# One-hots of the gate matrix in a PEER routing stage: from two engines with 8 tokens a batch to one engine with 16

## The reference, cut to what matters

```
q = (xb @ wq).reshape(PEER_BLOCK, PEER_HEADS, 2, PEER_DHALF)
s = jnp.einsum('thcd,hcnd->thcn', q, subkeys)            # 2 x 128 scores
sv, si = lax.top_k(s, PEER_TOPK)                         # 16 best of each half
cand = sv[:, :, 0, :, None] + sv[:, :, 1, None, :]
fv, fi = lax.top_k(cand, PEER_TOPK)                      # 16 best pairs
i1 = take_along_axis(si[:, :, 0], fi // PEER_TOPK)
i2 = take_along_axis(si[:, :, 1], fi % PEER_TOPK)
e = i1 * N_KEYS + i2                                     # expert number
g = jax.nn.softmax(fv, axis=-1)
a = jax.nn.gelu(jnp.einsum('thkd,td->thk', u_tab[e], xb))
y = jnp.einsum("thk,thkd->td", g * a, v_tab[e])
```

## Time and profile before

| what | value |
|---|---|
| median of 3 runs | 4247.77 us (4244.9 to 4252.57) |
| the profiled execution | 4249.34 us |
| its span | 4247.5 us |
| routing stage in the span | about 1096 to 1959 us |
| experts stage in the span | from 1959 us to the end |

### The profile page before, as it was taken

The page is one execution under the profiler, slowest core; times in us unless marked ns, Lnnn a source line. Parts: engine busy times, 40 slices in busy tenths (PEclk is TensorE's granted clock), DMA queues, the critical chain, the costliest instruction groups (busy, mean ns, idle before and its releaser), DMA issues.

```text
span 4247.5 us, 54962 instructions
## 1 busy us (share of the span) xinstructions
PE 3343.3 (79%) x20744; PEld 1998.0 (47%) x20744; DVE 2474.5 (58%) x4984; ACT 730.5 (17%) x1124; POOL 1327.8 (31%) x1103
## 2 busy tenths in 40 slices
PE   5899665888766566552778888889997899998998
PEld 2555552444665555541444344445453544444454
DVE  3110454443278888885877666666665666664445
ACT  2111232111001122221111121112121212111111
POOL 0000000000000333331554545554545465543442
PEclk8899776999877666666999999999999999999999
DMA  6211334322300222117888888898887898887882
GB/s 182 82 54 68 107 110 170 102 102 101 121 11 11 84 85 65 51 49 246 294 289 283 287 278 280 304 314 299 316 299 277 310 326 319 315 306 250 314 312 101
DMA packets 335811, 836.25 MB, mean 197 GB/s; under 512 B 43513, under 2 KB 148897, under 8 KB 331361
## 3 DMA queue, kind: packets, MB, share of 16 engines
q0 software_dynamic: 129024, 469.82, 31.8%
q1 hardware_dynamic: 206576, 363.62, 24.8%
HBM read 741.40 MB, written 93.19 MB: 196 GB/s over the span
## 4 chain that ended last, share of the span: by engine, by line
PE 23%; DMA 11%; DVE 6%; POOL 4%; DVEq 4%; issue 3%; SPq 1%; ACT 1%; POOLq 0%; ACTq 0%
PE experts_ps L1508 11%; PE experts_ps L1494 8%; DMA experts_ut<-in_uT 6%; DMA experts_v_rows<-in_v,picks_by_choice 5%; PE experts_ps L1525 4%; POOL experts_u_rows L1600 2%; DVEq L1712 2%; POOL experts_v_rows L1613 2%; DVE experts_ul L1646 2%; DVEq L1682 1%; DVE experts_hl L1685 1%; DVE experts_prod L1711 1%; ACT experts_uh L1552 1%; DVE experts_hf L1681 1%; DVE experts_hh L1683 1%
## 5 line engine op out<-in xcount | busy, mean ns | idle before, releaser
L1600 POOL DMA_INDIRECT experts_u_rows<-in_u_rows,picks_by_token x448 | 576.1, 1286 | 776.1 <-DVEq L1712 684.9
L1494 PE MATMUL experts_ps<-experts_xh,experts_uh 128*128 128x320 f16 x2048 | 614.5, 300 | 56.5 <-DMA experts_xl<-scratch_xl 27.2
L1494 PE MATMUL experts_ps<-experts_xh,experts_ul 128*128 128x320 f16 x2048 | 614.0, 300 | 0.0
L1494 PE MATMUL experts_ps<-experts_xl,experts_uh 128*128 128x320 f16 x2048 | 614.0, 300 | 0.0
L1508 PE MATMUL experts_ps<-experts_vh,experts_hh 128*128 128x512 f16 x1280 | 500.5, 391 | 99.9 <-issue 87.7
L1613 POOL DMA_INDIRECT experts_v_rows<-in_v,picks_by_choice x448 | 498.4, 1113 | 248.7 <-issue 125.9
L1711 DVE CUSTOM_DVE_ANT_0 experts_prod<-experts_u_rows,experts_x 128x1024 f16<-128x1024 f32 x448 | 545.8, 1218 | 24.8 <-issue 12.4
L1508 PE MATMUL experts_ps<-experts_vl,experts_hh 128*128 128x512 f16 x1280 | 498.6, 390 | 0.0
L1508 PE MATMUL experts_ps<-experts_vh,experts_hl 128*128 128x512 f16 x1280 | 496.8, 388 | 0.0
L1696 DVE SCALAR_TENSOR_TENSOR experts_y<-experts_ps,experts_y 128x512 f32<-128x512 f32 x320 | 221.0, 691 | 471.0 <-PE experts_ps L1508 458.3
L1525 PE MATMUL experts_ps<-experts_v_rows,experts_sel 128*32 128x512 f32 x1792 | 269.8, 648 | 131.7 <-DMA experts_v_rows<-in_v,picks_by_choice 129.3
(11 more groups left out here) (257 smaller groups left out, 5050.4 us busy)
## 6 DMA issues: line engine op xcount, KB each, us to landing
experts_ut<-in_uT SPq DMA_DIRECT2D x128, 512.0 KB
experts_vt<-in_v SPq DMA_DIRECT2D x128, 512.0 KB, 6.2
scratch_g<-route_gbuf SPq DMA_DIRECT2D x5, 8192.0 KB, 30.6
experts_g<-scratch_g SPq DMA_DIRECT2D x128, 320.0 KB, 4.8
scratch_z<-project_z SPq DMA_DIRECT2D x10, 1984.0 KB, 7.1
project_piece<-in_w_in SPq DMA_DIRECT2D x15, 1024.0 KB, 5.8
merge_w_piece<-in_w_merge SPq DMA_DIRECT2D x13, 1024.0 KB, 7.8
mix_za<-scratch_z SPq DMA_DIRECT2D x10, 960.0 KB, 5.6
```

What stands on the lines that cost most here:

```text
L1494: mm = pe.matmul(ps[:, A0 + k2 % 2, 0:W], w[:, e % 2, k, :], x[:, k, c * W:(c + 1) * W], start=k == 0 and j == 0, stop=k == KT - 1 and j == 2)
L1600: pool.indirect_dma_start(u_rows[:, k % RU], None, u_table, bass.IndirectOffsetOnAxis(ap=picks.by_token[:, b, j:j + 1], axis=0)).then_inc( ...
```

## The change

VectorE makes all four one-hot matrices of a batch. A batch has 16 tokens in four groups, so every operation has 2048 elements in each partition instead of 1024, a block has 8 batches instead of 16, and the loop goes round twice instead of four times. `hot_h` is gone: after `hot_l` is made from `hot_r`, `hot_r` is multiplied by `gh` in place. GpSimd has nothing left to do in this stage. A batch now fills all four PSUM banks (4 to 7), and the order in which banks are reused is the old one. In `top16` match-and-replace writes over the scores instead of into `rest`, which is gone. Semaphore counts follow the new sizes.

```diff
-BT, QT = 8, 4
+BT, QT = 16, 4
...
-        rest = s.sb("rest", [P, 2 * PH * KEYS])
...
-        hot_h, hot_l = s.sb("hot_h", [P, 2, G, KEYS, QT], F16), s.sb("hot_l", [P, 2, G, KEYS, QT], F16)
-        one, scrap = s.sb("one", [P, 1]), s.sb("scrap", [P, 1])
+        hot_l = s.sb("hot_l", [P, 2, G, KEYS, QT], F16)
...
                     def batch(b, half):
                         pe.wait_ge(hots_ready, d * batches + b + 1)
-                        pe.wait_ge(lows_ready, d * batches + b + 3)
                         for q in range(G):
-                            pe.wait_ge(g_read, (d * batches + b) * 2 + q + 1)
+                            pe.wait_ge(g_read, (d * batches + b) * G + q + 1)
                             for t in range(4):
-                                o = ps[:, 4 + 2 * half + q, t * P:(t + 1) * P]
-                                pe.matmul(o, hot_c[:, half, q, :, t], hot_h[:, half, q, :, t], start=True, stop=False)
+                                o = ps[:, 4 + q, t * P:(t + 1) * P]
+                                pe.matmul(o, hot_c[:, half, q, :, t], hot_r[:, half, q, :, t], start=True, stop=False)
...
-            @block.gpsimd
-            def _(pool):
-                pool.memset(one[:], 1.0)
-                pool.drain()
-                pool.sem_inc(lows_ready, 2)
-
-                def body(n, slot):
-                    if not SB <= n < NB:
-                        return
-                    d = n - SB
-
-                    def batch(b, half):
-                        pool.wait_ge(rows_ready, d * batches + b + 1)
-                        pool.tensor_tensor(scrap[:], one[:], one[:], ALU.mult)
-                        pool.tensor_tensor(hot_l[:, half], hot_r[:, half], spread(gl[:, bass.ds(b * BT, BT)]), ALU.mult)
-                        pool.drain().then_inc(lows_ready, 1)
-                    over_batches(pool, batch)
-
-                over_all(body)
...
-                        dve.match_replace(rest[j], values[j][:, 0:8], scores[j], LOWEST)
+                        dve.match_replace(scores[j], values[j][:, 0:8], scores[j], LOWEST)
...
-                        dve.wait_ge(g_full, (d * batches + b) * 2 + 2)
+                        dve.wait_ge(g_full, (d * batches + b) * G + G)
...
                         dve.tensor_tensor(hot_r[:, half], numbers, spread(col[:, 0, now]), ALU.is_equal)
-                        dve.drain().then_inc(rows_ready, 1)
                         dve.tensor_tensor(hot_c[:, half], numbers, spread(col[:, 1, now]), ALU.is_equal)
-                        dve.tensor_tensor(hot_h[:, half], hot_r[:, half], spread(gh[:, now]), ALU.mult)
+                        dve.drain()
+                        dve.tensor_tensor(hot_l[:, half], hot_r[:, half], spread(gl[:, now]), ALU.mult)
+                        dve.drain()
+                        dve.tensor_tensor(hot_r[:, half], hot_r[:, half], spread(gh[:, now]), ALU.mult)
                         dve.drain().then_inc(hots_ready, 1)
```

More of the change, by code:

```diff
@@ L1026, in route_stage @@
         pickT_full = s.sem("pickT_full")
-        rows_ready, lows_ready = s.sem("rows_ready"), s.sem("lows_ready")
         hots_ready, places_ready, places_moved = s.sem("hots_ready"), s.sem("places_ready"), s.sem("places_moved")
@@ L1082, in _ @@
             def _(pe):
-                pe.sem_inc(g_full, 4)
+                pe.sem_inc(g_full, 2 * G)
                 def queries(n):
@@ L1143, in _ @@
                 act.sem_inc(s_read, 1)
-                act.sem_inc(g_read, 4)
+                act.sem_inc(g_read, G)
                 act.sem_inc(g_stored, 16)
@@ L1177, in batch @@
                         for q in range(G):
-                            act.wait_ge(g_full, (d * batches + b) * 2 + q + 5)
+                            act.wait_ge(g_full, (d * batches + b) * G + q + 2 * G + 1)
                             act.wait_ge(const_loaded, 64)
-                            act.activation(gbuf[:, :, bass.ds(b * BT + 4 * q, 4)],
-                                           ps[:, 4 + 2 * half + q, :].rearrange("p (t i) -> p i t", t=4),
+                            act.activation(gbuf[:, :, bass.ds(b * BT + QT * q, QT)],
+                                           ps[:, 4 + q, :].rearrange("p (t i) -> p i t", t=4),
                                            ACT.Copy).then_inc(g_read, 1)
@@ L1210, in _, with top16 @@
                 dve.wait_ge(const_loaded, 64)
-                def top16(scores, rest, values, indices):
+                def top16(scores, values, indices):
                     n = len(scores)
@@ L1219, in top16 @@
                         dve.max_index(indices[j][:, 0:8], values[j][:, 0:8], scores[j])
-                        dve.match_replace(rest[j], values[j][:, 0:8], scores[j], LOWEST)
+                        dve.match_replace(scores[j], values[j][:, 0:8], scores[j], LOWEST)
                     dve.drain()
                     for j in range(n):
-                        dve.max(values[j][:, 8:16], rest[j])
+                        dve.max(values[j][:, 8:16], scores[j])
                     dve.drain()
                     for j in range(n):
-                        dve.max_index(indices[j][:, 8:16], values[j][:, 8:16], rest[j])
+                        dve.max_index(indices[j][:, 8:16], values[j][:, 8:16], scores[j])
                 def body(n, slot):
@@ L1231, in body @@
                     hc = range(2 * PH)
-                    top16([sc[:, j, :] for j in hc], [rest[:, j * KEYS:(j + 1) * KEYS] for j in hc],
+                    top16([sc[:, j, :] for j in hc],
                           [sv[:, j, :] for j in hc], [si[:, j, :] for j in hc])
@@ L1243, in body @@
                     dve.drain()
-                    top16([pair[:, h, :] for h in range(PH)], [rest[:, h * KEYS:h * KEYS + OCTETS * 8] for h in range(PH)],
+                    top16([pair[:, h, :] for h in range(PH)],
                           [fv[:, h, :] for h in range(PH)], [fi[:, h, :] for h in range(PH)])
@@ L1299, in body @@
                     choice = ps[:, 3, 0:2 * P].rearrange("p (c t) -> p c t", c=2)
-                    dve.wait_ge(lows_ready, d * batches + 2)
                     dve.wait_ge(const_loaded, 64)
```

## The result

The changed kernel takes 4116.2 us (median of 4 runs, 4108.9 to 4122.8) against 4246.3 us (4 runs, 4239.3 to 4252.6): a ratio of 0.9694, 95% interval 0.9669 to 0.9718. The forecast was 4124 us, in a range of 4105 to 4150 us. The measured gain is 130 us, the forecast one 124 us.

What follows compares the result with a forecast made beforehand. VectorE was taken to set the pace in routing, with hot_h waiting for GpSimd. A block's stretch falls from 71.3 to 46.5 us; five blocks save 124 us, giving 4124 us, range 4105 to 4150.

Steps and rivals of the forecast that it cites:

- Rivals 2 and 3: VectorE's products: one element a cycle, 4203 us, chance 0.06; or multiply itself 2.38 us, 4388 us, chance 0.03.
- Operations of 1.23 us: One-hot batch on VectorE: each of the four operations of 2048 elements takes 1.23 us.
- Closing gap: End of each one-hot batch on VectorE: stays 0.39 us, 0.70 where the loop branches.
- inner gaps: The two drains between operations of a one-hot batch on VectorE: 0.21 us each.
- The wait at the third batch: VectorE waits in each block for TensorE's matmuls of the first batch, as buffers alternate: costs 1.1 us.
- The stretch before: VectorE from a block's first one-hot to the next block's memset, in the kernel before: 71.3 us.
- the loop's branch: Where the batch loop branches back: gap of 0.70 us instead of 0.39, once in a block instead of three times.
- In place: Match-and-replace in the selection writes over its input: costs nothing, at most 17 us if overlap is lost.
- The exponential: ScalarE's exponential behind the queries: slack before VectorE's sum over it shrinks from 11.0 to 9.1 us.
- The store: Store of a block's gates: issued about 4.9 us after the memset, lands at 35.5 us, still covered.
- Rival 4: TensorE's queries fall to the low clock: 256 take 64 us, exponential late, about 4220 us; chance 0.03.
- rival 3: VectorE's multiply itself takes 2.38 us for 1024 elements, whatever GpSimd does: slower, 4388 us; chance 0.03.

Runs made afterwards that it cites:

- the version without drains: Changed kernel with its own buffer for the high product and no drains in a batch, operations signalling semaphores themselves: 4099.1 us, and 4085.4 us when measured again.
- the low product twice: Changed kernel with the product hot_l made twice in each batch, with its drain: 4162.9 us, ratio 0.9806 to the kernel before.
- the width alone: Changed kernel's batches of 16 tokens, but GpSimd still makes hot_l: 4202.9 us, ratio 0.9887 to the kernel before.

## Why the prediction was right

**Where the time is.** That a stage whose lines are not in the chain that ended last still counts in full is shown: the experts stage begins 128.5 us earlier and lasts as long as before within scatter, and a product more on VectorE costs 47 us.

**Why hot_h took 2.38 us.** The forecast read it as standing still until GpSimd's product was over. Three runs show it. Without GpSimd's product it takes 0.68 us. With GpSimd's product started behind it, it takes 0.68 to 0.69 us and `hot_r` is the one that waits. With starts some nanoseconds apart, the comparison `hot_c` takes 0.69 or 2.44 us, by which engine is ahead. Rivals 2 and 3, slow products on VectorE, are excluded: 1.22 to 1.23 us over 80 of them.

The prediction drew on a rule of the Trainium skill (SBUF — State Buffer, "Who interferes with whom"): the two engines exclude each other for a whole instruction, and the first to start wins. The traces agree, for comparisons as well as products and in both directions. Their number for it is a distance of 0.54 to 0.56 us between the two ends with 1024 elements and of 1.08 us with 2048, which matches an operation's 0.69 or 1.23 us less a fixed part of 0.15 us.

**The sum.** Operations of 1.23 us: 1.22 to 1.23. Closing gap 0.39: 0.39. The term furthest off is that of the inner gaps, 0.21 us forecast and 0.14 measured: 80 x 0.07 = 5.6 us. The wait at the third batch costs 1.4 us instead of 1.1, 1.5 us the other way, and it follows from the gaps: VectorE goes on 1374.53 - 1362.16 = 12.4 us after the first one-hot as forecast, but would have been ready at 11.0 us instead of 11.3. Two smaller ones nearly cancel. The stretch before is 71.5 us on average over the five blocks and not 71.3, some 0.8 us more gain; in the changed kernel the period over the loop's branch is 5.8 to 6.3 us, where the forecast had 0.31 us above the others, and two more periods of the last block are longer, some 1 us less gain, for which no cause was looked for. 124 + 5.6 - 1.5 = 128 us, and the five stretches of the two traces differ by 127.9 us, the starts of the experts stage by 128.5. The rest up to the 130 us between the medians is within scatter.

The other rule drawn on is that of the Trainium skill (VectorE: DVE Perf Modes, "The DRAIN you can't avoid"): a semaphore between operations costs nothing beyond the pipeline flush. Where an operation signals by itself, the traces agree: `hot_c` starts 1368.80 - 1367.66 = 1.14 us behind `hot_r` in the changed kernel, without an increment, and 1.14 us behind it in the version without drains, with one, both times 0.09 us before `hot_r` has ended. The prediction took the rule over to drain instructions, and there it gives too little: the inner gaps are 0.14 us and not 0.08, of which 0.07 goes with the address (the low product twice), and an increment on the drain makes them 0.19.

**What was costed at nothing.** In place: nothing, with a ratio of 1.0001. The exponential: a slack of 9.8 us where 9.1 was forecast. The store: 4.6 us behind the memset, forecast 4.9. Rival 4: 29.5 us for 256 queries, where the rival had 64, with a granted clock of 0.88 in that part of the block.

**The slower side** (rival 3) needed a product of more than 2.85 us for 2048 elements. With GpSimd out of the loop all took 1.22 to 1.23 us; only beside GpSimd's product did one take longer, 4.63 us, in the run with the width alone.

## What to carry to other kernels

Two engines that work side by side in the trace need not work at the same time. Where an operation takes much longer than one of its size beside it, look at the other engine's end: if it ends a fixed step behind it, at whatever start, it stood still, and work put on the second engine is work taken from the first. Then it can be right to give the busiest engine all of it, in fewer and wider operations, and to take the drains out by letting operations signal for themselves; what bounds that next is another engine's period or late start (here TensorE's), which should be worked out first.

## What was not expected of the hardware

GpSimd's own duration had a wait in it too: 1.89 us for 1024 float16 elements where it starts first, 2.40 behind a comparison of VectorE. And two engines of which one releases the other can start within a hundredth of a microsecond in either order, so that in one execution the same instruction takes 2.44 us in 14 of the 16 batches of the first block and 0.69 us in the other four blocks. A batch hardly changes by it: 4.33 and 4.29 us.
